# Splitting a PSUM reduce between ScalarE and VectorE, and spreading one more half batch of conditioning over the first FFN

## What is computed

```python
for l in range(2):
    mod = (silu(c) @ w_ada[l] + b_ada[l])                    # 2048 -> 6 x 2048
    sh1, sc1, g1, sh2, sc2, g2 = split(mod, 6)
    h = rms_norm(x) * (1 + sc1) + sh1
    z = h @ w_in[l]                                          # q, k, v, latent q and kv, gating
    mix = concat(diff_attention(z), latent_attention(z), spatial_gating(z)) @ w_out[l]
    x = x + g1 * mix
    h = rms_norm(x) * (1 + sc2) + sh2
    x = x + g2 * conv_ffn(h)                                 # up 2048 -> 11264, conv, silu gate, down 5632 -> 2048
```

## Time and profile before

| | |
|---|---|
| median of three runs | 2408.33 us (2405.02 to 2409.03) |
| profiled execution | 2408.03 us, span 2406.2 us |
| TensorE (PE) busy | 2317.5 us, 96% |
| VectorE (DVE) busy | 1833.9 us, 76% |
| ScalarE (ACT) busy | 1191.4 us, 50% |
| GpSimd (POOL) busy | 295.3 us, 12% |
| loaded from HBM | 592.42 MB, 247 GB/s over the span |

### The profile page before, as it was taken

The page is one execution under the profiler, slowest core; times in us unless marked ns, Lnnn a source line. Parts: engine busy times, 40 slices in busy tenths (PEclk is TensorE's granted clock), DMA queues, the critical chain, the costliest instruction groups (busy, mean ns, idle before and its releaser), DMA issues.

```text
span 2406.2 us, 37348 instructions
## 1 busy us (share of the span) xinstructions
PE 2317.5 (96%) x14736; PEld 2018.3 (84%) x14736; DVE 1833.9 (76%) x2585; ACT 1191.4 (50%) x1781; POOL 295.3 (12%) x437
## 2 busy tenths in 40 slices
PE   5789999999999999999999999999999999999999
PEld 2568888888888888888887799998888888888888
DVE  1547887879989999999998585667997667766675
ACT  1333664455653455435545366545555355544553
POOL 4231321221101111111131020001110000000000
PEclk8899999999999999999999999999999999999999
DMA  9998787968989999999996665435896566656654
GB/s 335 318 300 283 252 285 250 316 203 283 308 281 344 345 305 297 327 340 321 295 309 196 202 188 160 138 120 155 288 313 202 186 191 193 187 191 192 189 189 148
DMA packets 442462, 596.97 MB, mean 248 GB/s; under 512 B 24188, under 2 KB 381744, under 8 KB 442032
## 3 DMA queue, kind: packets, MB, share of 16 engines
q1 hardware_dynamic: 386592, 392.54, 50.8%
q0 software_dynamic: 55296, 201.35, 25.4%
q10 hardware_dynamic: 400, 0.71, 0.1%
HBM read 592.42 MB, written 2.10 MB: 247 GB/s over the span
## 4 chain that ended last, share of the span: by engine, by line
PE 85%; DVE 5%; DMA 4%; ACT 3%; issue 3%; POOL 1%; DVEq 0%; ACTq 0%; POOLq 0%
PE bank L1159 85%; DMA ada<-in_w_ada_dram 3%; DVE wlo L1742 1%; ACT whi L1489 1%; DVE acc L1736 1%; DMA raw<-in_w_in_dram 1%; ACT hx L1557 0%; DVE T L1824 0%; DVE r L1809 0%; POOL ada L1120 0%; DVE hx L1845 0%; PE bank L1458 0%; POOL first_ada L1120 0%; ACT sc_s L1610 0%; DVE xT L1790 0%
## 5 line engine op out<-in xcount | busy, mean ns | idle before, releaser
L1159 PE MATMUL bank<-hx,whi 128*128 128x512 f32 (+1 forms) x4480 | 1361.8, 364 | 4.5 <-DVE hx L1970 3.0
L1742 DVE TENSOR_TENSOR wlo<-raw,whi 128x1024 fp32r<-128x1024 f32 (+2 forms) x774 | 909.3, 1181 | 416.8 <-ACT whi L1489 416.3
L1159 PE MATMUL bank<-hx,wlo 128*128 128x256 f32 x3840 | 1087.9, 283 | 25.0 <-DVE hx L1845 20.4
L1489 ACT ACTIVATE whi<-raw 128x1024 fp32r<-128x1024 f32 (+2 forms) x774 | 780.6, 1017 | 664.3 <-PE bank L1159 544.0
L1159 PEld LDWEIGHTS bank<-hx,whi 128*128 128x128 f32 x4480 | 803.8, 190 | 143.6 <-issue 5.4
L1159 PEld LDWEIGHTS bank<-hx,wlo 128*128 128x128 f32 x3840 | 732.0, 191 | 39.9 <-issue 21.7
L1159 PE MATMUL bank<-mx,whi 128*128 128x512 f32 (+1 forms) x2096 | 613.1, 356 | 1.2 <-DVE xT L1791 1.2
L1159 PE MATMUL bank<-mx,wlo 128*128 128x256 f32 x1728 | 486.5, 282 | 2.5 <-DVE wlo L1742 2.5
L1159 PEld LDWEIGHTS bank<-mx,whi 128*128 128x128 f32 x2096 | 370.8, 189 | 61.0 <-issue 4.0
L1120 POOL DMA_DIRECT2D ada<-in_w_ada_dram x367 | 217.1, 593 | 1341.5 <-DVE acc L1736 956.9
L1159 PEld LDWEIGHTS bank<-mx,wlo 128*128 128x128 f32 x1728 | 327.8, 190 | 5.3 <-DVE wlo L1742 4.0
(11 more groups left out here) (172 smaller groups left out, 1342.7 us busy)
## 6 DMA issues: line engine op xcount, KB each, us to landing
ada<-in_w_ada_dram POOLq DMA_DIRECT2D x367, 512.0 KB, 5.7
raw<-in_ffn_w_up_dram SPq DMA_DIRECT2D x352, 512.0 KB, 4.8
raw<-in_ffn_w_down_dram SPq DMA_DIRECT2D x176, 512.0 KB, 4.3
raw<-in_w_in_dram SPq DMA_DIRECT2D x128, 512.0 KB, 4.7
raw<-in_w_out_dram SPq DMA_DIRECT2D x48, 512.0 KB, 4.0
first_ada<-in_w_ada_dram POOLq DMA_DIRECT2D x17, 512.0 KB, 17.7
raw<-in_w_out_dram SPq DMA_DIRECT2D x32, 256.0 KB, 3.5
raw<-in_mla_w_uq_dram SPq DMA_DIRECT2D x12, 384.0 KB, 4.0
```

Of the source, the lines that this page charges most:

```text
L1159: return pe.matmul(out_, lhsT, rhs, start=start, stop=stop, skip_group_check=True)
L1489: return act.activation(out_, in_, ACT.Copy)
L1742: i_ = tt(dst, src, high.bitcast(F32), ALU.subtract)
```

## The change

1. In the pairs of `TWO_PAIRS`, the step "copy" is done by two engines: ScalarE copies the bank's second half to z (it waits for the unit, as VectorE did), and VectorE waits for that copy (`z_half`) and adds the first half in place, which gives the bank back. 24 steps are touched. "addz" stays as it is.
2. The planner's target for the 194 slots of the first FFN is 11 batches instead of 10.5. In projection 1, `ada_over(11, 60)` stands as before and finds what the FFN has left of batch 10.

```diff
@@ ffn
             if p == 0:
                 self.ada_flush_for(6 * l + 6)
                 if l == 0:
-                    self.ada_over(10.5, 194)
+                    self.ada_over(11, 194)
@@ tables
+            elif t[0] == "copy" and t[2] in TWO_PAIRS:
+                number("z_half", t[1:])
@@ bass_trunk
-        tot_half = sem("tot_half")
+        tot_half, z_half = sem("tot_half"), sem("z_half")
@@ ScalarE
                     copy(z_of(pair, c_), pair_bank(pair, b)).then_inc(emptied_act, 1)
+                elif kind == "copy":
+                    l, pair, c_, ph = t[1:]
+                    b = wait_full(act, ("win", *t[1:]))
+                    copy(ch(z, 2 * pair + c_), b[:, S:2 * S]).then_inc(z_half, 1)
@@ VectorE
                 elif kind == "copy" and t[2] in TWO_PAIRS:
                     l, pair, c_, ph = t[1:]
-                    b = wait_full(dve, ("win", *t[1:]))
-                    dve.tensor_reduce(ch(z, 2 * pair + c_), b[:, 0:2 * S].rearrange("p (h n) -> p n h", h=2), AX_X,
-                                      ALU.add).then_inc(emptied_dve, 1)
+                    b = bank[plan.bank["win", *t[1:]]]
+                    dve.wait_ge(z_half, num["z_half", t[1:]] + 1)
+                    tt(ch(z, 2 * pair + c_), b[:, 0:S], ch(z, 2 * pair + c_), ALU.add).then_inc(emptied_dve, 1)
```

## The result

The changed kernel takes 2416.78 us (median of 11 runs, 2410.47 to 2422.21); the kernel before, on the same chip, 2408.59 us (11 runs, 2405.02 to 2411.49). The ratio is 1.0034 with a 95% interval of 1.0025 to 1.0042: slower by 6 to 10 us, where 2413.5 us, +5.2, was forecast. The profiled execution took 2416.96 us, 8.9 more than that of before.

What follows compares the result with a forecast made beforehand. TensorE (busy 2317.5 of 2406.2 us) was taken as the bound, with VectorE second in the first FFN, hidden by its lead. 2408.0 - 0.3 + 2.4 + 1.5 + 1.9 = 2413.5 us; range 2406 to 2419.

Steps and rivals of the forecast that it cites:

- forecast A: First FFN: VectorE's lead (weights split ahead of TensorE) exhausted in two or three places, +3 to +8 us; chance 0.44.
- signs: TensorE waits for wlo near 850-885, 1130-1150, in the last down pass; together 6 to 9 us against 2.5.
- Each further microsecond of VectorE is a microsecond of TensorE: First FFN: once VectorE's lead is gone, its added work costs TensorE the same time; each part is 1.19 us.
- Part 1: 24 copies in projection 1 and layer 0's first projection: one shows on TensorE near 102.6 us, -0.3 us (0 to -0.8).
- Part 2: First FFN, target 10.5 to 11: 158 parts instead of 144, paid out of lead; bounds 0 and 16.7 us.
- (a): Blocks 9 to 11: six more parts, 7.2 us, less 2.4 of filled gaps and 2.2 of lead; +2.4 us taken.
- (b): Blocks 16 to 21: six more parts, 7.2 us, less 2.4 of filled gaps and 3.1 of end lead; +1.5 us taken.
- (c): Last down pass of the first FFN: lives on lead, starts with up to 3.1 us less; +1.9 us (0 to 3.1).
- (d): Projection 1 loses 14 parts, 17 us of VectorE; its longest waits have no part in front of them: 0.
- rival D: Projection 1: parts taken out free its chains (waits for r, mqk); at most 5.4 us gained, 2402.6 us; chance 0.08.
- B, the loads: First FFN's fullest up blocks: loads become the bound, 3.8 us on top of forecast A, 2417 to 2421 us; chance 0.20.
- C, the lead holds: First FFN: free VectorE time takes in the added parts, +0 to +2 us, 2408 to 2410 us; chance 0.28.

Runs made afterwards that it cites:

- light work: The changed kernel with 15 FFN parts worked on by VectorE in 16 of 1024 columns, loads whole: 2410.15 us against 2408.03, ratio 1.0008.
- light loads: The changed kernel with the same 15 FFN parts loading only 16 of 1024 columns, VectorE's work whole: 2414.96 us against 2408.03, ratio 1.0031.
- The two runs that bear on it: Changed kernel with target 10.5 (copies only), ratio 1.0006; changed kernel with target 10, 1.0001, beside the kernel before with target 10, 1.0007.
- 11 alone: The kernel before with target 11 instead of 10.5, without the copies: 2415.54 us against 2408.03, ratio 1.003.
- more work on ScalarE: Changed kernel at target 10.5, four more small ScalarE copies ahead of each of the 24 copies: 2409.68 us against 2408.63, ratio 1.0005.

## Why the prediction was right or wrong

**The direction, the mechanism and the stage were right.** The forecast A (lead exhausted in two or three places) is what the trace shows, and the runs with light work and light loads show that it is VectorE's queue. The time, +8.2 us, lies just above A's +3 to +8 and inside the range. Of its signs the places came true (waits at 857 and 889, at 1139, and 3.0 us in the last down pass), the sum didn't: 5.5 us of waits for wlo, where 6 to 9 were named. "Each further microsecond of VectorE is a microsecond of TensorE" was meant as waits, and half of the loss isn't in them.

**Part 1** was put at -0.3. Its rows in the changed kernel, the tile z (ns min, median, max), which answer to the earlier trace rows, and TensorE's wait that answers to the earlier trace rows:
```profile
L1491 ACT ACTIVATE z<-bank x80: 359/383/598, 85.2 to 1532.8; 128x256 f32<-128x256 f32 x72, 128x512 f32<-128x512 f32 x8
...
L1762 DVE TENSOR_TENSOR z<-bank,z x24: 412/417/425, 86.5 to 1362.7; 128x256 f32<-128x256 f32 x24
...
102.39 1.12 PE L1344 MATMUL bank<-con,wsr 128*128 128x128 f32 x4 [2.84 <-DVE z L1762]
```
24 copies of 0.38 and 24 adds of 0.42 us, as priced. The wait is 2.84 us in place of 3.88, but it ends 0.20 us earlier; the rest is where it begins. The two runs that bear on it (1.0006, and 1.0001 beside 1.0007) allow from -2 to +4 us, so the sign of 0.3 us is open. What the Trainium skill (VectorE: DVE Perf Modes, Rules for kernel authors) says of tensor_reduce on a hot path would have given 6 us here. With a target of 10 the copies make VectorE 6.0 us lighter (busy for 1828.1 us against 1834.1), and the time doesn't move (1.0001 beside 1.0007): but for this one wait, these reduces were not on the path.

**Part 2, (a), blocks 9 to 11:** 2.4 taken, +2.0 in the pair of profiled executions. One execution scatters by more than the 0.4: with the same parts as before this stage took 180.75 and 182.53 us in two kernels, with those of after 182.83, 185.08 and 185.51. That the size fits so well is luck.

**(b), blocks 16 to 21:** 1.5 taken, +2.9 measured. This is the term that was mis-sized. I let the whole lead of 3.1 us at its end count as cover. Yet the wait at 1139.33 stands at the start of block 19, right behind the three fullest blocks (7, 7 and 8 parts), while the lead at the end is built again by blocks 19 to 21 (5 each), to 1.6 us at the start of the last down pass. What covers a block is the lead at that block, not the one at the end of the stage. The kernel before could have told: at the start of block 18, behind its 8 and 5 parts, its lead is already down to nothing, and the weight load waits:
```profile
1108.88 0.19 PEld L1159 LDWEIGHTS bank<-hx,wlo 128*128 128x128 f32 x1 [0.32 <-DVE wlo L1742]
```
And sixteen of its units run at 2.82 us, some 0.8 us, which the sum, made of waits alone, has no term for. Other executions with the same parts came out at +1.9 (11 alone) and +2.0 (light loads), so part of the +2.9 is this execution's own.

**(c), the last down pass:** 1.9 taken, +0.8 measured: the half between its bounds was too much, since the lead that it gets had recovered to 1.6 us, against 2.9 by the same measure in the kernel before. With the 0.5 us of the second down pass, which had no term, the stage comes to 6.1 against 5.8 predicted: the sum is nearly right because errors of both signs cancel.

**(d), projection 1:** 0 taken. Its first stretch is 1.4 us longer, within the scatter of 2, where 14 parts fewer stand, and the list of TensorE's waits, 1300 to 1660 us, has against the earlier trace rows
```profile
PE bank L1161 <- DVE r L1815: 1.4, 1, 1.4
PE bank L1161 <- DVE mqk L1892: 1.4, 2, 1.0
```
the waits that rival D wanted to end. D is down. That parts in projection 1 can cost something is still true: at a target of 9.5, with one every 5 us of VectorE's queue (37 from 1299.8 to 1491.2 us) where before there was one every 14 (14 from 1306.7 to 1484.4), the stretch is 4.1 us longer, 2.56 of them the wait near 1404.

**B, the loads.** What spoke for it was real, from 883 to 950 us of the changed kernel, against the earlier trace rows (median us to landing):
```profile
raw<-in_ffn_w_up_dram SPq DMA_DIRECT2D x24, 512.0 KB, 5.8
ada<-in_w_ada_dram POOLq DMA_DIRECT2D x15, 512.0 KB, 5.5
```
5.8 us where it was 5.2, and a DMA share of 0.98. But a load that lands 0.6 us later is not yet a wait of TensorE: with it back at 5.3 us (light loads) nothing was gained. **C, the lead holds,** fell too: at most 2 us were allowed, 6.1 were spent.

**Open:** of the 8.2 us between the medians, 6.1 are shown in the FFN. Of the 8.9 between the profiled executions, 4.4 stand ahead of the FFN and layer 1 gives 1.6 back. The 4.4 are no sign of the change: the kernel before and those with targets of 9.5, 10, 11 and 11.5 alone are the same program up to the first FFN, yet their first projection ends at 344.3, 342.1, 346.8, 344.2 and 348.6 us; in the changed kernel it ends at 348.7. 3.0 of the 4.4 come between 201 and 252 us, where the last section shows a half-speed spell. The run with the moved parts alone had 7.2 us in the FFN and 7.5 by its median. Whether the last microsecond or two belongs to the copies, to the clock or to scatter isn't settled.

## What to carry to other kernels

Where a second engine is busy for 94% of a stage, its free time is not a budget: follow its lead over the first engine, block by block, against the fullest blocks and not the mean. Of the first engine's lost time, its own list of waits showed half at most; compare the time of the same instructions too. Compare one pair of executions only after looking how far two executions of the same work lie apart. And a slower kernel with less work for VectorE on its page is no contradiction: what counts is in which stage the work stands, and the place with free time behind the stage can hold a chain that is hurt by it.

## What was unexpected of the hardware

TensorE can lose time without waiting, with its weights ready and its clock at full. The changed kernel behind its wait at 1139.33, then the kernel with light loads behind its wait of 1.10 us at 1139.42, the same 23 units:
```profile
1142.26:1208.29 66.03, 66.03 (x381) 56.96 (x380) 63.05 (x84) 35.27 (x52) 7.95 (x15) 1.00 0.94 311
...
1142.32:1207.57 65.25, 65.25 (x382) 56.83 (x380) 62.27 (x83) 35.88 (x53) 7.99 (x15) 1.00 0.92 298
```
In the first most units take 2.82 us, with leads up to 3 us; in the second 2.77, with shorter leads. The slower pace came in other kernels too, once over 16 units in a row of blocks 8 to 10 in the run with more work on ScalarE, where no wait stood ahead of it. What starts it isn't known.

The clock falls in one execution and not in another after the same wait. The changed kernel, TensorE after its wait of 1.98 us for r in layer 0, and the window around it:
```profile
230.85 1.97 PE L1161 MATMUL bank<-r,con 12*64 12x256 f32 x8 [1.98 <-DVE r L1815]
...
225.00:245.00 20.00, 18.02 (x117) 15.18 (x116) 13.70 (x15) 4.23 (x4) 2.26 (x3) 0.83 0.73 250
```
The kernel before, the same place, and the window of the kernel with a target of 10, the same program up to here:
```profile
230.59 1.08 PE L1159 MATMUL bank<-r,con 12*64 12x256 f32 x8 [1.98 <-DVE r L1809]
...
225.00:245.00 20.00, 18.02 (x143) 15.36 (x142) 15.96 (x19) 5.82 (x6) 2.37 (x4) 1.00 0.86 291
...
225.00:245.00 20.00, 18.03 (x120) 15.35 (x119) 13.76 (x15) 4.23 (x4) 2.27 (x3) 0.83 0.74 250
```
The granted clock is 0.83 of full speed over these 20 us in the first and the last, and 1.00 in the other: with levels of 1.2 and 2.4 GHz that is 6.8 us at the lower one, and eight matmuls took 1.97 us and not 1.08. TensorE was busy for 18.02 us in both of the kernels before and after, and made 117 matmuls in the one at the lower clock, 143 in the other. With a target of 11 the window has 0.91, with 9.5 it has 1.00. So the spell belongs to the execution and not to the change, and a difference of 3 us between two profiled executions needs a look at this column before it is explained.
